# Modulation of a four-layer transformer pair: six of ten late spans moved from TensorE matmuls to running scaled sums on VectorE

## The reference, cut to what matters

```python
sc = jax.nn.silu(c); sc_ctx = jax.nn.silu(c_ctx)
for l in range(DEPTH):                       # w_ada[l]: 2048 x 6144
    shift, scale, gate = jnp.split(sc @ w_ada[l] + b_ada[l], 3, axis=-1)
    shift_c, scale_c, gate_c = jnp.split(sc_ctx @ w_ada[l] + b_ada[l], 3, axis=-1)
    h_lat = rms_norm(x, norm_g[l]) * (1.0 + scale[:, None]) + shift[:, None]
    h_ctx = rms_norm(xc, norm_g[l]) * (1.0 + scale_c) + shift_c
    ...                                       # projections, attention, gates: h @ w_in
    x = x + gate[:, None] * merge_groups(..., w_out[l])
```

## Time and profile before

| | |
|---|---|
| median of three runs | 3137.79 us (3133.08 to 3138.83) |
| profiled execution, its own time | 3129.61 us |
| its span, first to last instruction | 3127.8 us |
| TensorE matmul busy | 2958.3 us, 95% |
| VectorE busy | 1587.0 us, 51% |
| ScalarE busy | 1021.5 us, 33% |
| mean granted TensorE clock | 0.977 |
| DMA | 501.94 MB, 160 GB/s on average |

### The profile page before, as it was taken

How to read it: one execution, slowest core, us unless ns; L and a number is a source line. 1 busy time by engine, 2 the same in 40 slices (tenths; PEclk the granted TensorE clock), 3 DMA queues, 4 the chain that set the end, 5 groups by cost and what they waited for, 6 DMA issues and landing times. The chain is left out here.

```text
span 3127.8 us, 41128 instructions
## 1 busy us (share of the span) xinstructions
PE 2958.3 (95%) x17192; PEld 2372.8 (76%) x17192; DVE 1587.0 (51%) x2512; ACT 1021.5 (33%) x1510; POOL 102.0 (3%) x157
## 2 busy tenths in 40 slices
PE   6899999999998999998999999999989989999988
PEld 2577777776776878886777778767767778798888
DVE  4334434356336544455563553555563365738574
ACT  3222243225113233334332222334441132225453
POOL 0000000000000000000000000430000000004000
PEclk9999999999998999999989999999999989999999
DMA  9644343231544555624745344323455433232455
GB/s 406 267 172 154 126 148 128 88 108 72 186 174 173 204 192 189 221 96 153 279 164 192 129 179 160 136 105 131 155 185 188 172 103 114 93 102 90 146 169 169
DMA packets 129161, 501.94 MB, mean 160 GB/s; under 512 B 14160, under 2 KB 39504, under 8 KB 104144
## 3 DMA queue, kind: packets, MB, share of 16 engines
q1 hardware_dynamic: 109104, 474.96, 42.6%
q10 hardware_dynamic: 19872, 24.35, 2.3%
HBM read 484.05 MB, written 8.39 MB: 157 GB/s over the span
## 5 line engine op out<-in xcount | busy, mean ns | idle before, releaser
L1420 PE MATMUL products<-h_high,w_high 128*128 128x512 f32 (+1 forms) x3424 | 1254.8, 366 | 92.0 <-DVE h_low L1012 30.9
L1420 PE MATMUL products<-h_low,w_high 128*128 128x512 f32 (+1 forms) x3424 | 1194.3, 349 | 0.0
L1420 PE MATMUL products<-h_high,w_low 128*128 128x512 f32 (+1 forms) x3424 | 1193.7, 349 | 0.0
L911 DVE TENSOR_TENSOR w_low<-w_raw,w_high 128x1024 fp32r<-128x1024 f32 x500 | 614.0, 1229 | 807.1 <-ACT w_high L589 803.6
L589 ACT CAST w_high<-w_raw 128x1024 fp32r<-128x1024 f32 x500 | 523.1, 1046 | 1384.8 <-PE products L1420 1243.8
L1420 PEld LDWEIGHTS products<-h_high,w_high 128*128 128x128 f32 x3424 | 662.2, 193 | 298.8 <-issue 151.0
L1420 PEld LDWEIGHTS products<-h_high,w_low 128*128 128x128 f32 x3424 | 662.4, 193 | 81.4
L1420 PEld LDWEIGHTS products<-h_low,w_high 128*128 128x128 f32 x3424 | 664.1, 194 | 78.3 <-issue 10.1
L1420 PE MATMUL products<-w_high,h_high 128*128 128x256 f32 x640 | 183.7, 287 | 5.4 <-DVE w_low L911 4.9
L1420 PE MATMUL products<-w_high,h_low 128*128 128x256 f32 x640 | 181.8, 284 | 0.0
L1420 PE MATMUL products<-w_low,h_high 128*128 128x256 f32 x640 | 181.8, 284 | 0.0
(11 more groups left out here) (217 smaller groups left out, 2610.6 us busy)
## 6 DMA issues: line engine op xcount, KB each, us to landing
w_raw<-w_slots SPq DMA_DIRECT2D x500, 512.0 KB, 3.5
ada_w<-ada_slots SPq DMA_DIRECT2D x168, 1024.0 KB, 7.6
mix_a<-ada_slots SPq DMA_DIRECT2D x12, 1024.0 KB, 14.5
mix_b<-ada_slots SPq DMA_DIRECT2D x12, 1024.0 KB, 15.2
x_scratch<-x_residual ACTq DMA_DIRECT2D x3, 2048.0 KB, 7.8
x_residual<-x_scratch ACTq DMA_DIRECT2D x3, 2048.0 KB, 9.3
x_residual<-x SPq DMA_DIRECT2D x1, 4096.0 KB, 13.4
x_residual<-x ACTq DMA_DIRECT2D x1, 4096.0 KB, 12.9
```

Of the source, the lines that this page charges most:

```text
L911: nc.vector.tensor_tensor(wlo[:, n % SPL, :], raw[:, n % RAW, :], whi[:, n % SPL, :].bitcast(F32), ALU.subtract).then_inc(low_done, 1)
L1420: ins = nc.tensor.matmul(o, a, b, start=first and q == 0, stop=last and q == 2, skip_group_check=skip)
```

## The change

Six spans, the gate of layer 0, shift and scale of layer 1, the gate of layer 2, and shift and scale of layer 3, are no longer units. Each is two blocks of 1024 columns, and each block 16 pieces of 128x1024 (512 KB), one for each 128 rows of the matrix. VectorE multiplies a piece by the condition's value of each row (one scalar per partition) and adds it to a running sum in `ada_w`, once for each of the two conditions: the first piece of a block with a tensor_scalar, the other 15 with a scalar_tensor_tensor. When a block is complete, TensorE sums each of the two accumulators over the partitions with 8 matmuls of one column against ones, 16 in all (`block_sums`), and VectorE adds the bias (`block_columns`). There are 12 blocks, 192 pieces and 384 VectorE instructions. The four other spans stay units: three in layer 1, and one, the gate of layer 3, in the stages `q` and `k` of layer 3. A string of digits per stage, `mod`, says how many pieces VectorE takes in each slot; all of them lie in layers 0 and 2. The diff, cut:

```diff
-OPEN_UNITS = 4 * (ADA_FIRST + 1)
-ADA_SPANS = ((0, 2),) + tuple((layer, part) for layer in range(1, LAYERS) for part in range(3))
+OPEN_UNITS = 4 * ADA_FIRST
+ADA_SPANS = ((1, 2), (2, 0), (2, 1), (3, 2))
+MOD_SPANS = ((0, 2), (1, 0), (1, 1), (2, 2), (3, 0), (3, 1))
...
+            linear("kv", layer, 1, ALL, "kv", "copy", "KV", ada=beside, mod=vec("11211110"), heads=all_stages({0: ("q", 3), 1: ("k", 0)}))
...
+            linear("g_gqa", layer, 2, toks, "feat", "gate", "Q", sync=True, ranks="cq", ada=beside, mod=vec("1111112111111200"))
...
+            ada = 2 if layer == 3 else 0
+            linear("q", layer, 2, toks, "feat", "copy", "G", heads=q_heads, ahead=5, ada=ada,
+                   mod=vec("0000000011111111"))
+            linear("k", layer, 2, ALL, "feat", "copy", "K2", ada=ada, mod=vec("1010101010101010"),
                    heads=all_stages({0: ("q", 3), 1: ("k", 0), 2: ("k", 1), 3: ("k", 2)}))
+            linear("v", layer, 2, ALL, "tok", "copy", "V2", mod=vec("2122121212012122"), heads=all_stages({0: ("k", 3)}))
+            linear("pool_v", layer, 2, toks, "feat", "copy", "Q", att=att, mod=vec("1101010101010100"))
+            linear("pool_g", layer, 2, toks, "feat", "gate", "Q", att=att, mod=vec("1010101010101011"))
+            linear("attn_g", layer, 2, toks, "feat", "gate", "G", sync=True, sub=True, mod=vec("0101010101010100"))
+        linear("out", layer, 4, toks, "feat", "res", "X", ada=4 if layer == 1 else 0, ahead=3,
+               mod="111111211111120" * 2 + "00" if layer in (0, 2) else "")
...
                 if n in SWAPS:
                     swap(*SWAPS[n])
+                for p in PIECES.get(n - 1, ()):
+                    piece(p)
+
+            def piece(p):                                  # SyncE
+                if p >= 2:
+                    sp.wait_ge(mod_used, p - 1)
+                if p < 2 or UNITS_DONE[p] > UNITS_DONE[p - 2]:
+                    sp.wait_ge(ada_used, UNITS_DONE[p])
+                sp.dma_start(mod_w[:, p % 2, :], dram["mod_slots"][p, :, :]).then_inc(mod_landed[p % 2], 16)
...
+            def pieces(n):                                 # VectorE, last in slot n
+                for p in PIECES.get(n, ()):
+                    b, chunk = p // KC, p % KC
+                    cond = 2 * (MOD_BLOCKS[b][0] // 2)
...
+                    dve.wait_ge(mod_landed[p % 2], 16 * (p // 2 + 1))
+                    if chunk > 0:
+                        dve.wait_ge(mod_used, p)
+                        own()
+                    for st in block_conds(b):
+                        w, c, acc = mod_w[:, p % 2, :], sc32[:, chunk, cond + st:cond + st + 1], mod_acc[:, st, :]
+                        if chunk == 0:
+                            ins = nc.vector.tensor_scalar(acc, w, c, None, ALU.mult)
+                        else:
+                            ins = nc.vector.scalar_tensor_tensor(acc, w, c, acc, ALU.mult, ALU.add)
+                        if st == 0:
+                            step(ins)
+                    ins.then_inc(mod_used, 1)
...
+            def block_sums(n):                             # TensorE, after slot n
+                if n - 1 not in BLOCK_END:
+                    return
+                b = BLOCK_END[n - 1]
+                pe.wait_ge(mod_used, KC * (b + 1))
...
+                for st in block_conds(b):
+                    for m in range(MOD_TILES):
+                        c = st * MOD_TILES + m
+                        ins = nc.tensor.matmul(AD[:, c:c + 1], mod_acc[:, st, m * P:(m + 1) * P], ONES[:, 0:1],
+                                               start=True, stop=True)
+                ins.then_inc(mod_col, 1)
```

More of the change, by code:

```diff
@@ L35 @@
 ADA_FIRST = 8
-ADA_QUADS = LAYERS * ADA_BLOCKS
 ADA_RING = 6
-OPEN_UNITS = 4 * (ADA_FIRST + 1)
-ADA_SPANS = ((0, 2),) + tuple((layer, part) for layer in range(1, LAYERS) for part in range(3))
+OPEN_UNITS = 4 * ADA_FIRST
+ADA_SPANS = ((1, 2), (2, 0), (2, 1), (3, 2))
+ADA_QUADS = ADA_FIRST + 4 * len(ADA_SPANS)
+MOD_SPANS = ((0, 2), (1, 0), (1, 1), (2, 2), (3, 0), (3, 1))
+MOD_COLS = 1024
+MOD_BLOCKS = tuple((layer, part, half) for layer, part in MOD_SPANS for half in range(2))
+MOD_TILES = MOD_COLS // P
 ADA_ORDER = (0, 4, 1, 5, 2, 6, 3, 7, 8, 9, 10, 11)
@@ L136, in plan_phases @@
             at["fd"] += 1
-            linear("g_gqa", layer, 2, toks, "feat", "gate", "Q", sync=True, ranks="cq", ada=1)
+            linear("g_gqa", layer, 2, toks, "feat", "gate", "Q", sync=True, ranks="cq", ada=beside, mod=vec("1111112111111200"))
             def count_ranks():
@@ L172, in plan_phases @@
             at["fd"] += 4
-            linear("pool_g", layer, 2, toks, "feat", "gate", "Q", ada=ada, att=att)
-            linear("attn_g", layer, 2, toks, "feat", "gate", "G", ada=ada, sync=True, sub=True)
+            linear("pool_g", layer, 2, toks, "feat", "gate", "Q", att=att, mod=vec("1010101010101011"))
+            linear("attn_g", layer, 2, toks, "feat", "gate", "G", sync=True, sub=True, mod=vec("0101010101010100"))
         add("ysplit", layer=layer, toks=toks)
-        linear("out", layer, 4, toks, "feat", "res", "X", ada=4 if layer < LAYERS - 1 else 0, ahead=3)
+        linear("out", layer, 4, toks, "feat", "res", "X", ada=4 if layer == 1 else 0, ahead=3,
+               mod="111111211111120" * 2 + "00" if layer in (0, 2) else "")
         if layer != 1:
@@ L324, in columns_ready @@
         def columns_ready(layer, parts):
-            return ADA_FIRST if layer == 0 and parts == 2 else \
-                ADA_FIRST + ADA_SPANS.index((layer, parts - 1)) + 1
+            if layer == 0 and parts == 2:
+                return ada_ready, ADA_FIRST
+            if (layer, parts - 1) in ADA_SPANS:
+                return ada_ready, ADA_FIRST + ADA_SPANS.index((layer, parts - 1)) + 1
+            return mod_ready, 2 * MOD_SPANS.index((layer, parts - 1)) + 2
         def span_of(quad):
@@ L417, in unit_place, with block_conds @@
             return ada_w[:, u % 2, :], ada_landed[4 + u % 2], OPEN_UNITS // ADA_RING + (u - OPEN_UNITS) // 2 + 1
+        PIECES, BLOCK_END, UNITS_DONE, BLOCKS_DONE = {}, {}, {}, {}
+        for ph in PH:
+            if ph["kind"] != "linear":
+                continue
+            if ph["ada"]:
+                BLOCKS_DONE[4 * ph["at"]["ada"]] = ph["at"]["mod"] // KC
+            p = ph["at"]["mod"]
+            for k, count in enumerate(map(int, ph["mod"])):
+                for _ in range(count):
+                    PIECES.setdefault(ph["at"]["slot"] + k, []).append(p)
+                    UNITS_DONE[p] = 4 * ph["at"]["ada"]
+                    if p % KC == KC - 1:
+                        BLOCK_END[ph["at"]["slot"] + k] = p // KC
+                    p += 1
+        OUT_FIRST = {ph["at"]["mod"] // KC: ph["at"]["slot"] for ph in PH
+                     if ph.get("name") == "out" and ph["layer"] == 0}
+        def block_conds(b):
+            return (0, 1) if MOD_BLOCKS[b][0] % 2 == 0 or MOD_BLOCKS[b][1] < 2 else (1,)
         def split_beside(pi, t, split):
@@ L506, in round_ @@
                                     slot(1)
-                            for u in range(4 * ADA_FIRST, OPEN_UNITS):
-                                unit(u)
                             return
@@ L511, in round_ @@
                             slot(n0 + 8 * i + k)
-                            if ph["name"] == "out" and ph["layer"] < 2 and i == 0 and k == 0:
+                            if ph["name"] == "out" and ph["layer"] == 1 and i == 0 and k == 0:
                                 sp.wait_ge(slot_used, n0)
@@ L781, in _ @@
                     layer = ph["layer"]
[L783 removed]
+                    act.wait_ge(*columns_ready(layer, 2))
                     for t in range(KC):
@@ L1688, in opening @@
                                 head_side(ph, 7)
-                        for u in range(4 * ADA_FIRST, OPEN_UNITS):
-                            span_unit(u)
                     def round_(i):
```

65 lines of the change are left out of this document (49 added, 16 removed).

## The result

The changed kernel takes 3156.06 us (median of 6 runs, 3151.18 to 3170.22), the kernel before 3136.58 in the runs beside it (6 runs, 3130.07 to 3138.83). The ratio is 1.0066, 95% interval 1.0051 to 1.0081: slower by 0.66%, outside the 0.2% that count as no change. The profiled execution of after is the longest of its six (3170.22, mean granted clock 0.958; the others stand at 0.962 to 0.966, those of before at 0.973 to 0.977). Single stages are therefore compared in the profiles, and totals by medians.

The account below looks back on a forecast made before the run. TensorE, busy 95% of the span, was taken as the bound. Terms -108.6 - 5.7 + 16.6 + 40.1 + 18.7 + 46 = +7 us gave 3137 for the profiled execution, 3145 for the median; range 3098 to 3178.

Parts of the forecast that it names:

- units, columns, units of layer 3: TensorE: 56 unit pairs gone, -108.6 us; seven spans' columns gone, -5.7; gate units moved into `k` of layer 3, +16.6.
- VectorE's lateness, loads with it: Layers 0 and 2: TensorE waits longer for VectorE's low parts, +46 us, bounds 15 and 85; late loads a separate rival.
- sums, with the clock: TensorE at block ends: 11 paid groups of one-column sums, +40.1 us, and half clock behind each, +18.7.
- pair and column prices: TensorE: a pair of units costs 1.94 us, the columns of a span 0.81 us.
- the lower bound of 8.6: `k` of layer 3: least cost in us of its gate units, four pairs at 1.94 plus columns at 0.81.
- `q`, put at nothing: `q` of layer 3: four pairs free in TensorE's idle time; 7.8 us if that idle time is gone.
- the two pool stages: `pool_v` and `pool_g`: a piece ahead of a product copy, beside GpSimd's pooling, makes attention weights late, +7 us.
- `out`: `out` in layers 0 and 2: two pieces meet product emptying twice in each; with smaller delays +4 us each, +8.
- the rest of layer 0: Behind the reciprocal in `kv` 2 us, two-piece slots beside attention 3, rank norm in `g_gqa` 2: +7.
- The head chain of `v`: First slots of `v`, layer 2: from reciprocal start R, swap at R + 21, low part at R + 35.8; +17 us together.
- The cover holds: Rival, 0.32: full clock behind the sums, small delays in `out` and `attn_g` taken up by them; -36 us, 3102.
- Loads come late too: Rival, 0.20: slot loads stand behind waiting piece loads on SyncE's queue; 20 two-piece slots at 1.5 us, +30, 3175.

Follow-up runs that it names:

- no pieces: The change without any work on the six spans (no piece loads, scaled sums or one-column sums; columns set to zero): 3028.6 us, 0.9653 of the kernel before.
- one sum a block: The change with only the first of each block's 16 one-column sums done: 3100.4 us, 0.9882 of the kernel before.
- thin pieces: The change with the scaled sums of all but a block's first piece on 8 of 1024 columns: 3114.6 us, 0.9925 of the kernel before.
- all three small edits: The change with sums in two halves, layer 2's last row swap one weight load earlier, and layer 3's gate units in `v`, not `k`: 3145.5 us.
- the sums in three parts: The change with a block's 16 sums split 5, 5 and 6 between products inside the slot at whose end they stood: 3180.4 us.

## Why the prediction was right

The sign was right, and the terms were right in kind: 3145 was said, slower with the greatest chance, and it is 3156. The size of the change was not: +7 us was said, and it is 20. The range, 3098 to 3178, was wide enough for a gain too, and slower had a chance of 0.45 only. Three steps can be priced by the kernels, each by a difference of ratios times 3137 us. Two of them were missed by 11 and by 26 us, in opposite directions; that these partly cancelled is luck.

| term | predicted | measured, and from which kernels |
|---|---|---|
| units, columns, units of layer 3 | -97.7 | -109, no pieces against before |
| VectorE's lateness, loads with it | +46 | +72, one sum a block against no pieces |
| sums, with the clock | +58.8 | +58, the change against one sum a block (15 of 16 sums) |
| sum | +7 | +21 |

**What is removed.** The pair and column prices held: `g_mla` of layer 0 lost four pairs and 8.1 us, and from the profile of before to the one without pieces layer 0 is 49.7 us shorter (49.0 by my prices) and layer 2 66.8 (65.3). Layer 3 is 14.8 longer (16.6), by two errors that nearly cancel. `k` was too dear: its two unit groups cost 11.7 us in the kernel without pieces (97.1 to 108.8) and 13.8 in the change, not 16.6. I had taken the whole difference between two layers, though layer 2 had other delays in it; in the first of these kernels the lower bound of 8.6 was the nearer. And `q`, put at nothing because TensorE's idle time was to cover its units, is not free: from the last product of layer 2 to the last of `q` it is 84.7 us before, 90.4 without pieces and 88.8 in the change (77.9 in its own window, where 75 was said). In the two profiles the whole step is -103; the other 6 us of -109 lie in how profiled executions stand to medians.

**The sums and the clock.** Right in size and in kind. Ten groups of the change last 3.6 to 4.3 us; two, of which half level covers most, last 5.8 and 6.8. The clock's part by the runs' own mean clocks is 22 us (0.964 against 0.971) with full pieces and 28 with thin ones (0.965 against 0.974), where I had 18.7. The Trainium skill (TensorE: Matmul & The Clock Gate, the part on the HAM clock gate) read as in the prediction, that an engine which is not left idle keeps its clock, would give none of this. The traces disagree: TensorE was busy for 3.50 of 3.50 us at 603.5 and the clock was 0.50 just after, and with one sum in place of 16 it stayed at 1.00.

**VectorE's lateness.** This is the term that was mis-sized, +72 for +46, though inside its bounds of 15 and 85. The kernel with one sum a block against the kernel without pieces shows it stage by stage in their profiles. `attn_g` is 4.5 us longer, for 7 predicted; the two pool stages 1.7 for 7 (only five scaled sums beside GpSimd's pooling were dearer, 1.4 to 2.1 us each, 2 us in all, where I had ten at 1 us); `k` 3.9 for 0. `v` of layer 2 is 17.1, for 17 predicted, but not as predicted: 12.0 of it is time without work, and the rest is busy time at a lower clock (0.93 against 1.00). The failed places are `out`, 12.2 and 10.3 us where I had 8 for both, and the rest of layer 0, 18 where I had 7. Windows of `out` in layer 0, without pieces and with them:

```profile
733.80:921.80 188.00, 182.44 (x809) 150.58 (x809) 81.15 (x107) 44.23 (x54) 0.00 (x0) 0.97 0.37 132
```
```profile
751.90:952.10 200.20, 188.89 (x813) 154.37 (x813) 155.19 (x175) 44.37 (x54) 0.00 (x0) 0.95 0.56 202
```

TensorE is not busy for 11.3 us against 5.6, and for the rest it is busy longer with all but the same work (188.9 us against 182.4), at a lower clock. One of the waits in this stage, and the products just behind it (the columns of the earlier trace rows):

```profile
775.50:778.50 3.00, 0.04 (x1) 0.04 (x1) 3.00 (x4) 1.04 (x1) 0.00 (x0) 1.00 0.91 325
779.10:782.50 3.40, 3.40 (x10) 2.63 (x9) 3.40 (x4) 1.04 (x1) 0.00 (x0) 0.50 0.81 314
```

That is the step I left out: I priced the clock behind the sums, and let a wait for VectorE cost only its own length. In layers 0 and 2, where all pieces lie, TensorE is without work for 125.5 us against 81.8, which is 44 us more and close to my 46. But it is also busy for 22 us more. Half-clock time in these two layers is 85 us against 58 (181 against 143 in the whole profiles); half of the 27 more, some 14 us, is an estimate of what it cost, of the 26 that my term was short by. The earlier trace rows had shown such a fall behind a wait and I used it only as a price. The one sum left in each block is another 3 us. How the rest divides, and what of it is ScalarE's late raw weights, is not shown.

**The head chain of `v`** went as worked out. VectorE's timeline, and SyncE's, which answer to the earlier trace rows:

```profile
1857.48 6.55 DVE L1029 RECIPROCAL tmp<-tmp 128x1024 f32<-128x1024 f32 x1 [1.48 <-ACT tmp L654]
...
1885.73 0.69 DVE L1203 TENSOR_TENSOR tmp<-pool_sums,rope_heads 128x512 f32<-128x512 f32 x1 [6.94 <-DMA pool_sums<-k_diff]
...
1887.66 5.04 DVE L1009 SCALAR_TENSOR_TENSOR ada_w<-ada_w,cond_silu 128x1024 f32<-128x1024 f32 x4
1892.63 1.22 DVE L963 TENSOR_TENSOR w_low<-w_raw,w_high 128x1024 fp32r<-128x1024 f32 x1
```
```profile
1875.11 2.90 SPq L516 DMA_DIRECT2D ada_w<-mod_slots  x2
1878.05 0.43 SPq L504 DMA_DIRECT2D w_raw<-w_slots  x1
1878.59 5.71 SPq L528 DMA_DIRECT2D pool_sums<-k_diff  x8
```

With R at 1857.48 the swap is issued from R + 21.1 (predicted 21) and the low part is done at R + 36.4 (predicted 35.8). TensorE's longest wait there was 7.5 us, not 9 to 13; two of 2.3 us stood ahead of it, 12.1 in all.

**The rivals.** "The cover holds" asked for full clock behind the sums, and that fell. "Loads come late too" was half true: SyncE waited 804 us for VectorE to free piece buffers (614.3 and 190.0 in its waits) and ScalarE's wait doubled, but the time stayed 19 us below that rival's. I had counted 20 slots with two pieces, and the masks have 23, which would put that rival 4 us higher still. I had also argued that a slot load has two slots of lead. In `v`, where nine slots have two pieces, that lead is used up: ScalarE waits 38.0 us for raw weights even with thin pieces, and 4.2 without any.

## What to carry to other kernels

When work moves from the engine that bounds a kernel to one that feeds it slot by slot, price each wait that arises twice: its length, and the products that run at half clock behind it. Put tiny matmuls where products stand between them and no wait is near, but count on little from it alone: here half of the falls went, the others grew longer, and 2 to 5 us were left. A load that waits for a slow engine's buffer holds back the loads behind it on an in-order queue. Do not count on a queue of its own before trying it: here the late loads came earlier and the kernel lost 7 us.

## What the runs showed of the hardware

- One-column fp32 sums keep TensorE busy by the profile and still lower the granted clock: at 11 of 12 groups of 32 records (3.6 to 5.8 us) it fell, for 3.4 to 10.2 us, at seven of them with no wait in the 12 us ahead. Halves of 16 records with products between them left it alone at six of the seven blocks with no such wait, and at none of the five with one; one sum in place of 16, with thin pieces, left it alone at all 12.
- A wait of TensorE of some 2 to 3 us can be followed by 3.4 us at half level in which it is busy all the time (a wait of 3.0 us at 775.5 us in the kernel with one sum a block). From 180 us to the end of layer 0, and from `k` of layer 2 to its end, the clock of that kernel falls 13 times; 11 of the falls have a wait of 0.8 to 8.0 us within the 12 us ahead, and the other two hold waits of 1.3 to 3.1 us.
- The scatter from run to run was larger in some kernels with more falls, though not in all: the kernel before spans 8.0 us over the 17 runs beside the one with all three small edits, which spans 26.8 over 12, with mean clocks of 0.962 to 0.970; the one with the sums in three parts spans 4.6 over 4. Edits of 5 us that a stage of the profile shows plainly could not be told in the median.
- A scaled sum of 128x1024 with two inputs took 1285 ns in the mean over 360 (1225 in the earlier trace rows), so the nearest row priced it to 5%.
